# One scan per pair in scan order, and kernel products of two pairs on two column tiles, in the S5 mixer of a two-layer diffusion backbone

## The reference, cut to what matters

```
for direction in range(2):
    lam_bar = exp(lam * dt)                                  # (32, 64), complex
    b_bar = ((lam_bar - 1.0) / lam)[..., None] * b
    order = identity if direction == 0 else flip over time
    bu_c = einsum('gpk,blgk->blgp', b_bar, order(uc))        # context
    x_c = ssm_scan(lam_bar, bu_c)                            # x[t] = lam_bar * x[t-1] + bu[t]
    bu_l = einsum('gpk,blgk->blgp', b_bar, order(ul))        # latents
    bu_l = bu_l.at[:, 0].add(lam_bar * x_c[:, -1])           # start from the context's last state
    x_l = ssm_scan(lam_bar, bu_l)
    ys_l += order(einsum('gkp,blgp->blgk', c_mat, x_l).real) # the same for ys_c
```

## Time and profile before

| | |
|---|---|
| median of 3 runs (1920.11 to 1926.1) | 1921.41 us |
| the profiled execution: device time, span | 1922.82 us, 1921.0 us |
| PE, DVE, ACT busy in the span | 95%, 64%, 38% |
| first rotation of pair 0 | at 473.24 us |
| steps 0 to 3, each | 23.9 us |
| steps 4 and 5, each | 21.5 us |
| step 6 | 20.5 us |
| step 7 begins; first product of retention head 1 | at 632.42 us; at 649.66 us |

### The profile page before, as it was taken

How to read it: one execution, slowest core, us unless ns; L and a number is a source line. 1 busy time by engine, 2 the same in 40 slices (tenths; PEclk the granted TensorE clock), 3 DMA queues, 4 the chain that set the end, 5 groups by cost and what they waited for, 6 DMA issues and landing times.

```text
span 1921.0 us, 25350 instructions
## 1 busy us (share of the span) xinstructions
PE 1833.4 (95%) x9680; PEld 1539.9 (80%) x9680; DVE 1220.0 (64%) x2020; ACT 728.3 (38%) x1003; POOL 62.6 (3%) x39
## 2 busy tenths in 40 slices
PE   6899999999889799999999999999999999989998
PEld 2688888877788587888888878888888797789998
DVE  4677677778999854777577357766333434755554
ACT  2522122336766833322132252312322434654343
POOL 0000000020000001000000100000002000010001
PEclk7999999999989998999999999999999999989999
DMA  7444545331110122554464235444223241034553
GB/s 298 154 175 157 188 183 209 120 113 66 45 45 28 39 72 104 186 202 148 148 235 146 94 129 192 172 153 178 95 77 113 107 176 55 2 111 174 179 183 120
DMA packets 39860, 257.81 MB, mean 134 GB/s; under 512 B 4688, under 2 KB 5840, under 8 KB 14832
## 3 DMA queue, kind: packets, MB, share of 16 engines
q1 hardware_dynamic: 39792, 256.92, 37.1%
HBM read 255.85 MB, written 1.05 MB: 134 GB/s over the span
## 4 chain that ended last, share of the span: by engine, by line
PE 84%; DVE 10%; ACT 3%; issue 2%; DMA 1%; SPq 0%; DVEq 0%; ACTq 0%
PE ps_all L1574 26%; PE ps_all L1578 25%; PE ps_all L1575 25%; DVE w_lo L924 2%; PE ps_all L1964 2%; PE bank L1622 1%; DMA start_scale<-in_w_scale 1%; PE bank L1977 1%; PE bank L2000 1%; ACT w_hi L538 1%; DVE cp L432 1%; DVE stat L1307 1%; PE bank L1789 1%; DVE wb L1238 0%; DVE normed L1294 0%
## 5 line engine op out<-in xcount | busy, mean ns | idle before, releaser
L1574 PE MATMUL ps_all<-a_hi,w_lo 128*128 128x512 f32 (+1 forms) x1800 | 663.4, 369 | 21.5 <-ACT a_hi L648 14.0
L1578 PE MATMUL ps_all<-a_lo,w_hi 128*128 128x512 f32 (+1 forms) x1800 | 657.4, 365 | 0.2 <-DVE a_lo L1063 0.2
L1575 PE MATMUL ps_all<-a_hi,w_hi 128*128 128x512 f32 (+1 forms) x1800 | 657.2, 365 | 0.0
L924 DVE TENSOR_TENSOR w_lo<-w_raw,w_hi 128x2048 fp32r<-128x2048 f32 (+3 forms) x184 | 376.5, 2046 | 162.1 <-ACT w_hi L538 160.9
L538 ACT ACTIVATE w_hi<-w_raw 128x2048 fp32r<-128x2048 f32 (+3 forms) x183 | 313.5, 1713 | 338.4 <-PE ps_all L1578 331.0
L1574 PEld LDWEIGHTS ps_all<-a_hi,w_lo 128*128 128x128 f32 x1800 | 345.5, 192 | 79.7 <-issue 16.2
L1578 PEld LDWEIGHTS ps_all<-a_lo,w_hi 128*128 128x128 f32 x1800 | 345.2, 192 | 56.8 <-DVE a_lo L1063 4.1
L1575 PEld LDWEIGHTS ps_all<-a_hi,w_hi 128*128 128x128 f32 x1800 | 345.8, 192 | 52.1 <-issue 0.2
L936 DVE SCALAR_TENSOR_TENSOR mod_junk<-mod_raw,cond 128x1024 bf16<-128x1024 f32 x256 | 302.7, 1220 | 5.4 <-ACT cond L566 2.7
L1574 PE MATMUL ps_all<-g_hi,w_lo 128*128 128x512 f32 (+1 forms) x704 | 258.4, 367 | 1.0 <-DVE w_lo L924 1.0
L1578 PE MATMUL ps_all<-g_lo,w_hi 128*128 128x512 f32 (+1 forms) x704 | 258.3, 367 | 0.0
(11 more groups left out here) (236 smaller groups left out, 1512.0 us busy)
## 6 DMA issues: line engine op xcount, KB each, us to landing
w_raw<-in_tiles SPq DMA_DIRECT2D x118, 1024.0 KB, 4.8
mod_raw<-in_w_mod SPq DMA_DIRECT2D x64, 1024.0 KB, 4.8
w_raw<-in_tiles SPq DMA_DIRECT2D x32, 768.0 KB, 4.1
w_raw<-in_tiles SPq DMA_DIRECT2D x32, 640.0 KB, 3.7
start_raw<-in_w_mod SPq DMA_DIRECT2D x4, 1024.0 KB, 16.1
start_scale<-in_w_scale SPq DMA_DIRECT2D x4, 1024.0 KB, 20.2
bias<-in_na_bias SPq DMA_DIRECT2D x2, 1536.0 KB, 8.9
cond<-in_cond SPq DMA_DIRECT2D x2, 1024.0 KB, 6.0
```

What stands on the lines that cost most here:

```text
L924: nc.vector.tensor_tensor(w_lo[:, slot, 0:size], w_raw[:, slot, 0:size], w_hi[:, slot, 0:size].bitcast(F32), ALU.subtract).then_inc(lo_rea ...
L1574: pe.matmul(dst, w[1], x[0], start=start, stop=False)
L1575: pe.matmul(dst, w[0], x[0], start=False, stop=False)
L1578: return pe.matmul(dst, w[0], x[1], start=False, stop=stop_)
```

## The change

- All four series of a pair (two directions, real and imaginary) are scanned by one instruction over 512 columns. Its rates are no longer one number broadcast, but a tile `rates` of 512 columns that holds 0 in the first column of each series, so that the carry is cut there. ACT writes it, once per pair (`scan_rates`, two instructions of 2 x 127 columns); GpSimd writes the zeros once.
- The backward direction stays in the order in which it is scanned, from the input product on: PE reads the tokens of each half in reversed order (`in_scan_order`), the table of steps counts up for both directions (so `const` loses 128 columns), and the states are written to `xs` with two instructions of 256 columns and no small ones. `outputs` reads the backward states reversed.
- `build_c` computes four powers per direction in place of five. Power 0 is written by ACT (`present_outputs`, four instructions of 64 columns per step).
- `kernel_products` works for both pairs of a step at once: pair 0's products go to partitions 0 to 31 of `ps_sum`, pair 1's to 32 to 63, in turn. It also waits for `present`.

```diff
-                    nc.vector.tensor_copy(pows[:, 0, 0::2, :], powers[:, 0, 0])
+                    nc.vector.tensor_copy(pows[:, 0, 0::2, :], powers[:, 0, 0, :, 1:5])
...
-                c = c_in[:, p, qd, :].rearrange("p c (a k) -> p c a k", a=1).broadcast_to([P, 4, 5, 16])
+                c = c_in[:, p, qd, :].rearrange("p c (a k) -> p c a k", a=1).broadcast_to([P, 4, 4, 16])
...
+                def present_outputs(b):
+                    act.wait_ge(S["pads"], 1)
+                    if b >= 2:
+                        act.wait_ge(S["y"], 2 * b - 2)
+                    for ri in range(2):
+                        for g in range(2):
+                            at = slice(64 * g, 64 * g + 64)
+                            ins = nc.scalar.activation(cp[at, b % 2, :, ri, 0::9, 16 * g:16 * g + 16],
+                                                       c_in[at, ri, 4 * b:4 * b + 4, :].rearrange("p (q d) k -> p q d k", d=2),
+                                                       ACT.Copy, scale=1.0 if ri == 0 else -1.0)
+                    ins.then_inc(S["present"], 1)
+                def scan_rates(pair):
+                    if pair >= 2:
+                        act.wait_ge(S["scan"], pair - 1)
+                    for d in range(2):
+                        ins = nc.scalar.activation(rates[:, pair % 2, d, :, 1:P],
+                                                   ones[:, 1:P].rearrange("p (a j) -> p a j", a=1).broadcast_to([P, 2, P - 1]), ACT.Copy,
+                                                   scale=r4[:, 2 * pair + d:2 * pair + d + 1])
+                    ins.then_inc(S["rates"], 1)
...
                 angles(0)
+                present_outputs(0)
+                scan_rates(0)
+                scan_rates(1)
                 split_hi(base + 1, 2048, 1)
...
                         angles(b + 1)
+                        present_outputs(b + 1)
                         turned(2 * b + 2)
                         turned(2 * b + 3)
...
+                    if b < 7:
+                        scan_rates(2 * b + 2)
                     gelu(2 * b)
                     if b < 7:
                         sines(b + 1)
+                        scan_rates(2 * b + 3)
...
-                    for ri in range(2):
-                        ins = nc.vector.tensor_tensor_scan(zs[:, 1, ri, 63::-1], r[1].broadcast_to([P, 64]),
-                                                           rot[:, 0, 1, ri, 63::-1], 0.0, mul, add)
-                    ins.then_inc(S["half"], 1)
-                    for ri in range(2):
-                        nc.vector.tensor_tensor_scan(zs[:, 0, ri, :], r[0].broadcast_to([P, P]),
-                                                     rot[:, 0, 0, ri, :], 0.0, mul, add)
-                    dve.wait_ge(S["half"], pair + 1)
-                    for ri in range(2):
-                        ins = nc.vector.tensor_tensor_scan(zs[:, 1, ri, 127:63:-1], r[1].broadcast_to([P, 64]),
-                                                           rot[:, 0, 1, ri, 127:63:-1], zs[:, 1, ri, 0:1], mul, add)
-                    ins.then_inc(S["scan"], 1)
+                    dve.wait_ge(S["rates"], pair + 1)
+                    nc.vector.tensor_tensor_scan(sq_acc[:], rates[:, slot].rearrange("p d r j -> p (d r j)"), scaled[:, 0],
+                                                 0.0, mul, add).then_inc(S["scan"], 1)
...
-                        nc.vector.tensor_tensor(flat[:, to:to + XS_D + 65:XS_D + 64], b[0], b[1], op)
-                        x_to = x[:, :, ri * 130:ri * 130 + 130].rearrange("p d (b j) -> p d b j", b=2)[:, :, :, 0:64]
-                        ins = nc.vector.tensor_tensor(x_to, back[:, 0, :, ri, :], back[:, 1, :, ri, :], op)
+                        ins = nc.vector.tensor_tensor(xs[:, pair % 2, :, ri, 1:P + 1], back[:, 0, :, ri, :], back[:, 1, :, ri, :], op)
...
+                def in_scan_order(x, d):
+                    return x.rearrange("p (b j) -> p b j", b=2)[:, :, ::-1] if d else x
...
-                def kernel_products(pair):
+                def kernel_products(b):
                     pe.wait_ge(S["c"], b + 1)
+                    pe.wait_ge(S["present"], b + 1)
...
+                    to = [ps_sum[32 * ql:32 * ql + 32] for ql in range(2)]
                     for ri in range(2):
-                        pe.matmul(ps_sum[0:32, at:at + 96], bwd[ri], state_rows(c[ri][:, 6:9]), start=(ri == 0), stop=(ri == 1))
+                        for ql in range(2):
+                            pe.matmul(to[ql][:, 0:96], bwd[ql][ri], state_rows(c[ql][ri][:, 6:9]), start=(ri == 0), stop=(ri == 1))
```

More of the change, by code:

```diff
@@ L75 @@
 COLUMNS = 2 * CHUNKS + 76
-XS_D = 262
 MAGIC = 1.5 * 2 ** 23
@@ L326, in program @@
         s5_sem = {n: sem("s5_" + n) for n in (
-            "rows", "loads", "skip", "act", "tanh", "sin", "b", "pads", "us_act", "wprod", "w", "cprod", "c",
-            "ang", "magic", "frac", "abs", "tables", "turned", "vt", "v", "kmm", "k", "rot", "z", "half", "scan",
+            "rows", "loads", "skip", "act", "tanh", "sin", "b", "pads", "us_act", "wprod", "w", "cprod", "c", "present",
+            "ang", "magic", "frac", "abs", "tables", "turned", "vt", "v", "kmm", "k", "rot", "z", "rates", "scan",
             "back", "x", "y", "gelu")}
@@ L1739, in kernel_products @@
                     for ri in range(2):
[L1740 to L1742 removed]
+                        for ql in range(2):
+                            pe.matmul(to[ql][:, 96:224], fwd[ql][ri], state_rows(c[ql][ri][:, 0:4]), start=(ri == 0), stop=False)
@@ L1744, in outputs @@
+                    for ri in range(2):
+                        for ql in range(2):
+                            pe.matmul(to[ql][:, 96:128], bwd[ql][ri], c[ql][ri][:, 9, :], start=False, stop=False)
+                    for ql in range(2):
+                        pe.matmul(to[ql][:, 96:128], const[0:32, C_IDENT:C_IDENT + 32], skip[:, 2 * b + ql, :],
+                                  start=False, stop=True).then_inc(S["kmm"], 1)
                 def outputs(pair):
```

80 lines of the change are left out of this document (31 added, 49 removed).

## The result

The changed kernel took **1904.1 us** (median of 5 runs, 1902.11 to 1904.39) beside 1920.11 us for the kernel before on the same chip (5 runs, 1917.33 to 1926.1). The ratio is 0.9909, 95% interval 0.9895 to 0.9923. The profiled execution took 1904.13 us, of which the span is 1902.4: 18.6 us less than the span of before.

What follows compares the result with a forecast made beforehand. DVE was taken to bound first rotation to `fraction(7)`, ACT from there to head 0's mask. 8.5 + 3.2 - 0.7 - 0.8 + 0.15 = 10.3 us off 1921.41 gave 1911.1 us, range 1907 to 1917.5.

Steps and rivals of the forecast that it cites:

- the scan's term: On DVE, one scan of 512 columns takes 1.15 us in place of 1.62: 0.47 us less per pair, 14 pairs.
- DVE per pair: Scan 0.47 us less and state writes 0.14 less, 0.61 together; 14 pairs up to `fraction(7)` give 8.5 us.
- The straight line through two short scans: Scan price from 64 and 128 columns: 159 ns fixed plus 1.875 ns per column, so 1119 ns for 512.
- The rule that was weighed against it: Built-in scan at half throughput: long scan 1.38 us, 0.26 above the line, 3.6 us less gain in 14 pairs.
- DVE per step: `build_c` instructions shrink from 320 to 256 columns: 0.53 us less per call, 3.2 us for six calls.
- ACT: Added `scan_rates` take 0.8 us per pair, just covered by waits within steps; 0.8 us lost behind `fraction(7)`.
- the rival that ACT becomes the bound: Rates at 1.3 us a pair make ACT late; 4.5 to 6 us of gain lost, 1916.5 us; chance 12%.
- the tables: DVE waits 0.1 to 0.15 us for ACT's tables at the ends of steps 4 and 5.
- the split: In step 5 DVE waits 0.6 us for ACT's weight split; with the tables, 0.7 us lost together.
- TensorE: Column tiles save 1.2 us per step in `kernel_products`, worth nothing on the path; TensorE stays ahead by 1 us or more.
- The start: `const`, loaded ahead of the scale tiles, is 64 KB smaller: 0.15 us gained.
- The bound of 1.6 us in the prediction: Upper bound for the long scan: four scans of 128 columns, 159 ns paid each time; 6.6 us less gain.

Runs made afterwards that it cites:

- pad_both: Changed kernel with unused SBUF per partition, 512 bytes behind `const` and 64 behind `stat`, restoring the old addresses from `h` on: 1909.48 us, ratio to before 0.9951.
- rates_first: Changed kernel with the odd pair's rates made on ACT ahead of the sines instead of behind them: 1903.32 us, ratio to before 0.9908.
- before_g_low: Kernel before the change with `half_pi` and `magic` moved into `columns`, so `g_hi`, `g_lo` and all behind `columns` lie 64 bytes lower: 1913.46 us, ratio 0.9963.

## Why the prediction was wrong in size

**The step that failed** is the scope: the prediction took it that a change in the S5 part leaves every other stretch as it is, and costed the smaller `const` by its transfer alone (0.15 us). The smaller buffers move the operands of the feed-forward blocks, and 48 of their tiles got 7.0 us faster. With the distances of before (pad_both) the ratio is 0.9951, 9.4 us of gain (6.5 to 12.5) where 10.3 were forecast; 1921.41 less 9.4 is 1912.0, inside the range. No row of before could have given the size, since every down tile there has the same pace. But the fact that addresses move was in the diff, and the sum had no term and no rival for it. Nor had it one for TensorE's clock behind the mask, where head 1's faster scores give 0.4 us up to head 3's. That the S5 part comes near its forecast is in small part luck: the scan's term was 1.5 us too large (below), and this 0.4 stands against it.

**DVE per pair.** Writes 0.14 less, as forecast. The scan 1.62 to 1.26: 0.36 less, not 0.47. The straight line through two short scans gave 1.12 us for 512 columns; measured are 1.22. From 128 columns (399 ns) to 512 (1225) it is 2.15 ns a column, from 64 to 128 it had been 1.875. Some 1.4 to 1.5 us of the gain went there in 14 pairs. The rule that was weighed against it says that the scan runs at half throughput (the Trainium skill, "DVE: opcode table, instruction layouts, handler registers and perf-mode slots", section "Datapath and trigger behaviour"). The trace agrees for the part that goes by columns: a plain instruction of 512 columns takes 0.69 us, and a tiny one 0.17; the difference taken twice and the 0.17 once are 1.21. The fixed part is not doubled; 1.38 us, the rule taken to its end, is too much, by 0.16 us where the line was 0.11 too low. Means of all 16, by shape, after, 465 to 640 us (count, busy us, mean ns, idle):

```profile
L1301 DVE TENSOR_TENSOR_SCAN sq_acc<-rates,scaled 128x512 f32<-128x512 f32 x16 | 19.6, 1225 | 0.5
```

**DVE per step.** 3.2 us forecast for `build_c` in six calls. The call in the opening takes 3.21 us (462.64 to 465.85) in place of 1.72 + 2.02 = 3.74: 0.53 less, as forecast.

**ACT.** The rates take 0.89 us for a pair where 0.8 was forecast, and lie where they were expected. Timeline of ACT, after, a step with rope and the last one:

```profile
530.92 0.63 ACT L740 ACTIVATE tcos<-tsin 128x512 f32<-128x512 f32 x1 [0.97 <-DVE tsin L1283]
...
533.40 0.71 ACT L743 ACTIVATE tcos<-tcos,half_pi 128x512 f32<-128x512 f32 x1
534.01 0.89 ACT L732 ACTIVATE rates<-ones,r 128x254 f32<-128x254 f32 x2
534.93 1.02 ACT L696 ACTIVATE qk<-ps_all 128x1024 f32<-128x1024 f32 x1
```

```profile
615.23 0.63 ACT L740 ACTIVATE tcos<-tsin 128x512 f32<-128x512 f32 x1 [0.97 <-DVE tsin L1283]
...
617.71 0.70 ACT L743 ACTIVATE tcos<-tcos,half_pi 128x512 f32<-128x512 f32 x1
618.33 0.89 ACT L732 ACTIVATE rates<-ones,r 128x254 f32<-128x254 f32 x2
619.23 1.28 ACT L701 ACT_TABLE_LOAD   x1
...
632.97 0.80 ACT L792 ACTIVATE prod<-lag,columns,cond_k 128x512 f32<-128x512 f32 x1
633.67 0.61 ACT L795 ACTIVATE sq<-sq 128x512 f32<-128x512 f32 x1
```

ACT waits 0.97 us for the fraction, so it was not late, and the rival that ACT becomes the bound didn't come. DVE's waits for it are 0.7 us at the tables (three, 0.2 each) and 0.3 at the split, against 0.7 forecast in all. Behind the last sines the chain is unbroken, and 0.77 us longer (17.67 to 18.44), against 0.8 forecast; rates_first takes exactly that back.

**The sum in its place.** Loop 155.55 to 145.90, chain +0.77: 8.9 us gained. The forecast's terms, without the start, were 8.5 + 3.2 - 0.7 - 0.8 = 10.2; with the scan at its measured price they are 14 x 0.50 = 7.0, so 8.7.

**TensorE.** It reads the backward order at no cost, timeline of PE, after (input products of one pair, then output products):

```profile
595.56 1.05 PE L1730 MATMUL bank<-us,sq 128*128 128x128 f32 x8
...
596.67 1.06 PE L1769 MATMUL bank<-stat,cp 128*128 128x128 f32 x8
```

Half of each eight read in reversed order, and they take the 1.06 us of the earlier trace rows. It keeps a slack of up to 1.5 us a step ahead of `kernel_products`, where "1 us or more" was forecast, and the tiles are worth nothing, as forecast.

**The start** gave 0.4 us in the profiled execution (22.63 to 22.24) where 0.15 was forecast. Neither is shown: the same product starts at 22.31 in before_g_low, which loads the larger `const`, and between 22.05 and 22.69 in the variants of the changed kernel.

## What to carry to other kernels

A change that resizes a buffer changes the addresses of everything declared behind it, and with it possibly the pace of work that it never touches. Fill the hole with a pad first and time both: without that, 5 to 7 of these 17 us would have been credited to the scan. Where the trace holds only short forms of an instruction, a line through them is not a price for one four times as long: it was 0.11 us too low. The rule on throughput, taken to its end, was 0.16 too high; the two together would have bounded the price. And time taken off one engine can come back as another engine's clock: look at what waits behind the place that was shortened.

## What the runs showed of the hardware that was not expected

- Products of 128x512 (fp32r) follow at 229 or 233 ns in the down tiles and at 226.7 (10.88 / 48) or 233.3 (11.20 / 48) in the up tiles, at a granted clock of 1.00, depending on where the moving operand and the weights lie relative to each other. 64 B per partition make the difference (32 B do too, in the down tiles), and it is worth 7 us in the down tiles; a placement with slow up tiles as well brought the changed kernel to 1927.37 us from 1904.1. Which property of the distance decides is open.
- Four scans of 128 columns, 399 ns each in the profile before, take 1.37 us in a row when none waits for another: they follow at some 0.32 us. The bound of 1.6 us in the prediction paid the whole duration each time and was too high.
- The granted clock differs from trace to trace in places that have the same work. In the mixer's opening (0.87 or 1.00, worth 1.6 us) and in head 3's scores (0.59 before, 1.00 after) nothing here says why. In head 1's scores it goes with the wait ahead of them in all fourteen traces: 0.51 to 0.55 behind 3.44 to 3.85 us, 1.00 behind 2.29 to 2.77. In the profiled executions before and after, these places moved the span by 3.7 us, of which at most the 0.4 of head 1 belong to the change.
